# Query and key head norms of a hybrid decoder layer: squares summed as 4-byte floats in one matmul per half, instead of as a high and a low part in two

## The reference, cut to what matters

```python
def rms_norm(x, gain):
    xf = x.astype(jnp.float32)
    y = xf * lax.rsqrt(jnp.mean(xf * xf, axis=-1, keepdims=True) + EPS)
    return (y * gain.astype(jnp.float32)).astype(x.dtype)

def swa_sink_mixer(q, k, v, q_gain, k_gain, sinks):
    """q: (B, S, ATTN_WIDTH); k, v: (B, S, KV_WIDTH); returns (B, S, ATTN_WIDTH)."""
    ...
    q = rms_norm(q.astype(f32).reshape(B, S, ATTN_KV_HEADS, ATTN_GROUP, ATTN_HD), q_gain) * (ATTN_HD ** -0.5)
    k = rms_norm(k.astype(f32).reshape(B, S, ATTN_KV_HEADS, ATTN_HD), k_gain)
    ...
    scores = jnp.einsum('bnqhgd,bnkhd->bnhgqk', qb, kb)
```

## Time and profile before

| | |
|---|---|
| time, median of 3 runs | 1193.39 us (1191.31 to 1194.09) |
| the profiled execution: its time | 1192.22 us |
| the profiled execution: span from first to last instruction | 1190.4 us |
| PE busy | 1130.2 us |
| DVE busy | 709.5 us |
| ACT busy | 502.9 us |
| POOL busy | 464.6 us |
| mean granted clock of TensorE | 0.981 |

### The profile page before, as it was taken

The page is one execution under the profiler, slowest core; times in us unless marked ns, Lnnn a source line. Parts: engine busy times, 40 slices in busy tenths (PEclk is TensorE's granted clock), DMA queues, the critical chain, the costliest instruction groups (busy, mean ns, idle before and its releaser), DMA issues.

```text
span 1190.4 us, 14627 instructions
## 1 busy us (share of the span) xinstructions
PE 1130.2 (95%) x5532; PEld 931.9 (78%) x5532; DVE 709.5 (60%) x863; ACT 502.9 (42%) x772; POOL 464.6 (39%) x355
## 2 busy tenths in 40 slices
PE   4999999999999999978799999999999989999998
PEld 4998766678888788756688888888888867888876
DVE  7404588596859895759543333324243377777786
ACT  6314456644554631435333333333333254454531
POOL 6301124362433330221535454454535453343552
PEclk8999999999999999989799999999999989999999
DMA  6101100010103202320134322333133385445433
GB/s 248 53 1 36 54 19 2 22 50 19 36 18 125 84 1 94 114 81 18 53 115 133 101 101 82 115 115 115 58 111 133 142 303 191 140 152 165 133 105 146
DMA packets 37094, 112.63 MB, mean 95 GB/s; under 512 B 4897, under 2 KB 9761, under 8 KB 35617
## 3 DMA queue, kind: packets, MB, share of 16 engines
q1 hardware_dynamic: 37024, 111.71, 27.4%
HBM read 83.12 MB, written 28.57 MB: 94 GB/s over the span
## 4 chain that ended last, share of the span: by engine, by line
PE 76%; DVE 10%; ACT 4%; issue 4%; POOL 3%; DMA 2%; SPq 0%; DVEq 0%; ACTq 0%; POOLq 0%
PE ps L1205 23%; PE ps L1207 22%; PE ps L1206 22%; PE ps L1390 4%; PE ps L1349 1%; DVE olo L1825 1%; DVE ulo L1593 1%; PE ps L1362 1%; DVE B L1719 1%; PE ps L1221 1%; POOL D L698 1%; DVE vlo L1587 1%; DVE M L1752 1%; POOL sc L670 1%; DMA araw<-wd 1%
## 5 line engine op out<-in xcount | busy, mean ns | idle before, releaser
L1205 PE MATMUL ps<-ubhi,adhi 128*128 128x512 f32 x308 | 121.6, 395 | 8.1 <-DVE yacc L1898 6.5
L1206 PE MATMUL ps<-ublo,adhi 128*128 128x512 f32 x308 | 120.9, 392 | 0.0
L1565 DVE TENSOR_TENSOR glo<-graw,ghi 128x1024 fp32r<-128x1024 f32 x21 | 26.8, 1276 | 147.4 <-POOL s34raw L613 147.4
L1205 PE MATMUL ps<-uhi,whi 128*128 128x512 f32 x272 | 112.1, 412 | 0.0
L1207 PE MATMUL ps<-uhi,wlo 128*128 128x512 f32 x272 | 106.3, 391 | 0.0
L1206 PE MATMUL ps<-ulo,whi 128*128 128x512 f32 x272 | 106.1, 390 | 0.0
L698 POOL TENSOR_TENSOR D<-B 128x1024 f32<-128x1024 f32 x28 | 64.3, 2295 | 43.0 <-DVE M L1752 23.7
L711 POOL TENSOR_TENSOR hst<-sg,up 128x512 f32<-128x512 f32 x21 | 27.9, 1328 | 132.2 <-issue 66.4
L1205 PE MATMUL ps<-ohi,s34hi 128*128 128x512 f32 x168 | 66.8, 398 | 10.6 <-ACT ps L1041 10.6
L1205 PEld LDWEIGHTS ps<-ubhi,adhi 128*128 128x128 f32 x308 | 58.4, 190 | 23.1 <-DVE yacc L1898 7.8
L1898 DVE TENSOR_TENSOR yacc<-ps,yacc 128x512 f32<-128x512 f32 x104 | 68.8, 682 | 10.0 <-PE ps L1207 9.9
(11 more groups left out here) (281 smaller groups left out, 3046.9 us busy)
## 6 DMA issues: line engine op xcount, KB each, us to landing
hidden<-hst SPq DMA_DIRECT2D x11, 1792.0 KB, 8.2
ubraw<-hidden SPq DMA_DIRECT2D x33, 512.0 KB, 5.3
graw<-wg SPq DMA_DIRECT2D x21, 512.0 KB, 4.1
uraw<-wu SPq DMA_DIRECT2D x21, 512.0 KB, 3.4
wraw<-wproj SPq DMA_DIRECT2D x17, 512.0 KB, 3.5
araw<-wd SPq DMA_DIRECT2D x22, 384.0 KB, 4.3
x<-xT SPq DMA_DIRECT2D x8, 512.0 KB, 6.9
h<-xT SPq DMA_DIRECT2D x8, 512.0 KB, 4.6
```

What stands on the lines that cost most here:

```text
L1205: nc.tensor.matmul(out, whi_, xhi_, start=first, stop=False, skip_group_check=seeded)
L1206: nc.tensor.matmul(out, whi_, xlo_, start=False, stop=False, skip_group_check=seeded)
L1565: nc.vector.tensor_tensor(glo[g % 2][:, :], graw[g % 2][:, :], ghi[g % 2][:, :].bitcast(F32), ALU.subtract)\
```

## The change

The squares are no longer split. ACT squares each half into `asq` in 4 bytes as soon as that half is evacuated, and PE sums a half with a single matmul of 4-byte floats, with the stationary matrix `blk` in 4 bytes. POOL's squares, DVE's subtraction, the copy `blkr` and the step `AD` go. `AM` then stands where `AD` stood in the mixes, and the other steps are laid out anew.

```diff
     for u in range(5):
-        order += mix(proj([u]), [[("AD", u - 1)], [("AM", u - 1)], [("AN", u - 1)], [("AH", u - 1)], [("AL", u - 1)]]
+        order += mix(proj([u]), [[("AM", u - 1)], [("AN", u - 1)], [("AH", u - 1)], [("AL", u - 1)]]
                      if u else [], lead=2)
         order += [("AS", u)]
-    order += mix(take(6), [[("AD", 4)], [("AM", 4)], [("AN", 4)], [("AH", 4)], [("AL", 4)]], lead=1)
+    order += mix(take(6), [[("AM", 4)], [("AN", 4)], [("AH", 4)], [("AL", 4)]], lead=1)
...
             for step in order:
-                if step[0] == "AS":
-                    i = step[1]
-                    pool.wait_ge(s_pev, 2 * i + 2)
-                    if i >= 2:
-                        pool.wait_ge(s_asl, i - 1)
-                    nc.gpsimd.tensor_tensor(asq[:, i % 2, :], kq[:, i, :], kq[:, i, :], ALU.mult).then_inc(s_asq, 1)
-                elif step[0] == "SN":
+                if step[0] == "SN":
...
                 elif kind == "AS":
                     i = step[1]
-                    if i == 0:
-                        act.wait_ge(s_setup, 1)
-                        nc.scalar.activation(blkr[:, :], blk[:, :], ACT.Copy).then_inc(s_blk, 1)
-                    act.wait_ge(s_pev, 2 * i + 2)
-                    if i:
-                        act.wait_ge(s_ass, 2 * i)
-                    nc.scalar.activation(asqhi[:, :], kq[:, i, :], ACT.Square).then_inc(s_ash, 1)
+                    for half in range(2):
+                        act.wait_ge(s_pev, 2 * i + half + 1)
+                        if i >= 2:
+                            act.wait_ge(s_ass, 2 * i - 3 + half)
+                        t = slice(half * HALF, (half + 1) * HALF)
+                        nc.scalar.activation(asq[:, i % 2, t], kq[:, i, t], ACT.Square).then_inc(s_ash, 1)
...
                 elif kind == "AM":
                     i = step[1]
-                    pe.wait_ge(s_asl, i + 1)
                     if i == 0:
-                        pe.wait_ge(s_blk, 1)
+                        pe.wait_ge(s_setup, 1)
                         pe.wait_ge(s_vev, 2 * NC)
                     else:
                         pe.wait_ge(s_aln, i)
                     for half in range(2):
                         t = slice(half * HALF, (half + 1) * HALF)
-                        nc.tensor.matmul(ps[:, 3 + half, :], blkr[:, :], asqhi[:, t], start=True, stop=False)
-                        nc.tensor.matmul(ps[:, 3 + half, :], blkr[:, :], asqlo[:, t], start=False, stop=True)\
+                        pe.wait_ge(s_ash, 2 * i + half + 1)
+                        nc.tensor.matmul(ps[:, 3 + half, :], blk[:, :], asq[:, i % 2, t], start=True, stop=True)\
                             .then_inc(s_ass, 1)
...
-                elif kind == "AD":
-                    i = step[1]
-                    dve.wait_ge(s_asq, i + 1)
-                    dve.wait_ge(s_ash, i + 1)
-                    nc.vector.tensor_tensor(asqlo[:, :], asq[:, i % 2, :], asqhi[:, :].bitcast(F32), ALU.subtract)\
-                        .then_inc(s_asl, 1)
```

More of the change, by code:

```diff
@@ L199, in build @@
         blk = at("blk", 1, [P, P])
-        blkr = at("blkr", 1, [P, P], F32R)
         wmask = at("wmask", 1.5, [P, 2 * P])
@@ L249, in build @@
         asq = at("asq", 167, [P, 2, T])
-        asqhi, asqlo = at("asqhi", 175, [P, T], F32R), at("asqlo", 179, [P, T], F32R)
         pT = at("pT", 179, [P, 2, GRP * P])
@@ L343, in build @@
         s_pmm, s_pev, s_ufree = sem("proj_group"), sem("proj_evac"), sem("u_tiles_free")
-        s_blk, s_ash, s_asl = sem("blk_ready"), sem("an_sq_hi"), sem("an_sq_lo")
-        s_asq, s_ass, s_aln, s_ars, s_an = sem("an_sq"), sem("an_sum"), sem("an_ln"), sem("an_rstd"), sem("an_done")
+        s_ash = sem("an_sq")
+        s_ass, s_aln, s_ars, s_an = sem("an_sum"), sem("an_ln"), sem("an_rstd"), sem("an_done")
         s_kqhi, s_kqlo = sem("kq_hi"), sem("kq_lo")
```

## The result

| | median | lowest to highest | runs |
|---|---|---|---|
| before | 1191.68 us | 1189.48 to 1196.12 | 22 |
| changed | 1194.98 us | 1192.02 to 1198.38 | 22 |

The changed kernel takes 1.0026 times as long as the kernel before, with a 95% interval from 1.0017 to 1.0036. That is 2.0 to 4.3 us more, around 3.1 us. The mean of the two is 1.0019, or 2.3 us; the forecast was 2.13 us (1.0018). The three runs that the forecast started from had a median of 1193.39 us for the kernel before; over 22 runs it is 1191.68 us.

The account below looks back on a forecast made before the run. PE was taken as the bound, busy 1130.2 of 1190.4 us. Costlier sums in units 0 to 3 (3.24 us) less unit 4's gain (1.11 us) gave +2.13 us, so 1193.39 became 1195.5 us, range 1193.0 to 1198.0 us.

Parts of the forecast that it names:

- The bound: Head norms, 92 to 152 us: PE runs without gaps except at unit 4's sums, so added PE work lengthens the kernel.
- The price of a 4-byte sum: Head-norm sums on PE: one 4-byte matmul takes 0.86 us, so a unit's sums take 1.72 us against 0.91 us.
- a price per record: Rival at the sums: a 4-byte matmul costs two records of 0.23 us, giving 1191.5 us; chance 0.04.
- The stall: PE's 1.80 us wait at unit 4's sums goes, with 0.66 us of slack; unit 4 gains 1.11 us.
- T + 5.53: Start of `kqn` for unit 4, counted from T, when PE is through with unit 4; no new wait at the scores.
- The sum: Whole change: 3.24 us added less 1.11 us gained, +2.13 us at 152 us.
- units 0 to 3: Sums of these four units on PE: 0.81 us more each, 3.24 us in all, none hidden by gaps.
- Nothing found behind the scores: After PE's first scores, forecast at 154.1 us, everything moves as one block, with 1038.4 us to the end as before.
- The side of 0.2%: Whole kernel: 0.18% slower, just inside the 0.2% (2.4 us) that can't be told from no change.
- The stall that stays: Rival at unit 4's sums: ACT's second square is late and PE waits again, up to 1197.4 us; chance 0.12.
- the absorbed shift: Rival behind the scores: a wait PE doesn't start swallows up to 2.13 us, giving 1193.4 us; chance 0.04.
- The clock: Rival behind later PE gaps: less low clock gives 1191.0 us, chance 0.07; more gives 1197.5 us, chance 0.07.

Follow-up runs that it names:

- the pair twice: Kernel before, with each half's two float32r sum matmuls issued twice into the same bank, stall left in: 1.0039 [1.0026, 1.0052] of before.
- the kernel by halves: Kernel before, split kept, with ACT's and POOL's squares and DVE's subtraction made per half: 0.9973 of before, and 0.9980 when repeated.
- The first measurement: The changed kernel timed against the kernel before, 22 runs each: 1.0026 [1.0017, 1.0036].
- the second measurement: The changed kernel, unaltered, timed once more against the kernel before on another occasion: 1.0012 [1.0001, 1.0023].
- the kernel with the places of before: Changed kernel with an empty step where the subtraction stood, so the sums stand behind as many parts as before: 1.0010 [0.9999, 1.0021] of before.

## Why the prediction was right

**The bound.** PE is dense here and everything else lies beside it: shown by the pair twice (+4.53 us in the stretch, and 3.1 to 6.2 us in the time).

**The price of a 4-byte sum.** 0.86 us, by the distance between starts, against a price per record: shown in the changed trace (1.72 us for two) and by issuing the sums twice.

**The stall.** It is gone. The second square ended 0.66 us before its matmul was due, as worked out. The forecast had `kqn` at T + 5.53 and `kqlo` done by T + 9.3; with unit 4's end at T = 143.23, they came at T + 5.52 (148.75) and T + 9.24. What the stall is worth with its restart (1.92 us beside float32r sums) is shown in part by the kernel by halves, which got back 1.42 us of it and lost the rest to a new wait of PE at the same place.

**The sum.** +2.13 us forecast, +2.36 us in the trace. The term that was mis-sized is that of units 0 to 3: it was put at 3.24 us, and the distances between their sums grew from 11.79 us to 12.65 us, which is 0.86 us each or 3.44 us. I had priced the 4-byte matmuls alone. About a dozen ordinary matmuls behind each pair of them are 0.005 us slower, 0.05 us per unit. The rows for it stood in the trace of before (the earlier trace rows show one such place, and I subtracted 0.23 us there without asking why it wasn't 0.227).

**Nothing found behind the scores.** The landmarks to 307 us move with the scores. The forecast of the first scores at 154.1 us was 0.5 us early: 0.2 us is the term above, and 0.3 us is the later start of unit 0. From the first scores to the end it took 1038.45 us before, and 1039.1 and 1037.8 us in two traces of the changed kernel, so the sign of the difference there isn't even the same.

**The side of 0.2%.** The forecast was 0.18%, just within the bound. The first measurement lies above the bound with 1.0026, the second below it with 1.0012, and the stretch says 0.20%. So what was measured doesn't settle on which side of 0.2% the change lies. That it makes the kernel slower rests on the stretch, which has the same 2.36 us each time, and on both intervals, of which the second excludes no change only just (1.0001). How much of the 2.36 us arrives at the end is less sure: the two intervals together reach from 0.1 to 4.3 us, and the kernel with the places of before, with the same stretch, has an interval that takes in no change.

**The luck in the median.** The forecast of 1195.5 us was 0.5 us above the measured 1194.98 us, closer than its parts were. It stood on a median of three runs that was 1.7 us above the one of 22 runs, and on a difference of 2.13 us where the medians differ by 3.30 us; the two errors nearly cancel. What bears out the prediction is the stretch, not this number.

**The rivals.** The stall that stays, the price per record and the absorbed shift are refuted by the runs above. The clock moved from one execution to the next as feared (0.91 against 1.00 in 400 to 420 us), but in no direction that goes with the change: over the runs of the second measurement its mean was 0.984 with the change and 0.985 before.

**Open.** The kernel by halves was timed 3.2 and 2.4 us below before, where its stretch gives 1.42 us. Behind the scores it took 1034.1 and 1036.6 us in its two traces, where the other kernels took 1036.4 to 1040.6 us. Whether that is scatter or something that its timing does to the later gaps of PE wasn't settled. Why ordinary matmuls are a little slower behind two 4-byte ones but not behind four, and behind a wait, also stays open.

## What to carry to other kernels

Where PE is the bound, a 4-byte matmul (0.86 us) pays on PE only if it replaces about four float32r ones (0.227 us each) or a stall as long as the difference; here it replaced two, and the work that it took from POOL and DVE cost nothing except for one stall. Before paying on the bound engine to be rid of a wait, ask whether the waited-for work can simply start earlier: making the same squares and subtraction by halves took most of the stall away at no cost to PE, and gave the fastest of the measured kernels that sum the whole square (0.9973 and 0.9980 of before). And read a price from distances between starts, taking in a dozen of the instructions behind it.

## What the runs showed of the hardware

POOL's product of 128x512 4-byte numbers took 1.04 us alone and 1.42 us when DVE's subtraction with two operands in SBUF (0.68 us, started 0.16 us earlier) ran beside it; keeping them apart brought it back to 1.04 us in all ten cases. The Trainium skill (SBUF — State Buffer, section SBUF: two separate sides) says that such a DVE operation and a GpSimd operation that reads SBUF lock each other out of a shared pair of ports for a whole instruction, whichever starts first. The trace agrees that the later one, POOL, is held up. It doesn't show a full block: DVE's subtraction ran 0.52 us into POOL's product, which took only 0.38 us longer.

Behind a pair of 4-byte sums the ordinary matmuls start 0.232 us apart for about a dozen, then 0.227 us again. Behind four 4-byte sums in a row they start 0.228 us apart, and behind float32r sums, even eight in a row, 0.226 to 0.227 us apart.
